# GpSimd multiplications with a second factor of 1.0, and a key bias by multiplication and addition, in a two-layer decoder kernel

## What is computed

```python
def trunk_layer(...):
    h = einsum('btd,de->bte', x, w_in)              # one projection, 4168 columns
    u = cc * ch                                     # mixer A: gated convolution, 256 channels
    conv = conv_w[0] * u_full[:, 0:t]
    for i in range(1, 3):
        conv = conv + conv_w[i] * u_full[:, i:i + t]
    y_a = cb * conv * silu(cg)
    y_b = stick_breaking(...) * silu(sg)            # mixer B: 6 heads x 64
    y_c = dsa_attend(...) * silu(dg)                # mixer C: 6 query heads, 2 kv heads
    x_new = layer_norm(ALPHA * x + concat(y_a, y_b, y_c) @ w_out)

def dsa_attend(...):                                # mixer C, per block of 128 queries
    score = ...                                     # indexer
    _, idx = top_k(where(admissible, score, -inf), 256)
    logits = where(valid, q @ gathered_k * HEAD_DIM ** -0.5, -inf)
    p = softmax(logits)
    o = p @ gathered_v
```

## Time and profile before

| what | value |
|---|---|
| time, median of 3 runs | 4671.03 us (4669.49 to 4673.32) |
| time of the profiled execution | 4666.6 us |
| span of the profiled execution | 4664.9 us |
| PE busy | 4315.7 us (93%) |
| DVE busy | 3508.5 us (75%) |
| ACT busy | 1737.3 us (37%) |
| POOL busy | 1472.1 us (32%) |
| POOL in the chain that ended last | 4% |

### The profile page before, as it was taken

The page is one execution under the profiler, slowest core; times in us unless marked ns, Lnnn a source line. Parts: engine busy times, 40 slices in busy tenths (PEclk is TensorE's granted clock), DMA queues, the critical chain, the costliest instruction groups (busy, mean ns, idle before and its releaser), DMA issues.

```text
span 4664.9 us, 79623 instructions
## 1 busy us (share of the span) xinstructions
PE 4315.7 (93%) x29678; PEld 2450.8 (53%) x29678; DVE 3508.5 (75%) x5659; ACT 1737.3 (37%) x2538; POOL 1472.1 (32%) x1393
## 2 busy tenths in 40 slices
PE   8988999999999898889999889999999998988899
PEld 6433545754466666454464235457544666655543
DVE  2785999999799774554537859999997997746445
ACT  3552212211266776330035522122112677754300
POOL 4310145400055795110033101454001647941100
PEclk9998999999899999999999989999999999999999
DMA  2102210211232003885211021112112320039832
GB/s 80 30 17 64 62 24 30 78 51 52 84 115 63 27 29 97 286 282 169 93 48 31 18 65 59 23 32 78 52 52 95 102 65 24 29 118 296 274 118 90
DMA packets 343763, 396.99 MB, mean 85 GB/s; under 512 B 100311, under 2 KB 264242, under 8 KB 340050
## 3 DMA queue, kind: packets, MB, share of 16 engines
q1 hardware_dynamic: 318034, 375.10, 25.6%
q10 hardware_dynamic: 25344, 16.79, 1.3%
HBM read 297.71 MB, written 94.14 MB: 84 GB/s over the span
## 4 chain that ended last, share of the span: by engine, by line
PE 72%; issue 6%; DVE 6%; ACT 6%; POOL 4%; SPq 2%; DMA 2%; ACTq 2%; DVEq 0%; PEldq 0%; POOLq 0%
PE banks L884 20%; PE banks L887 13%; PE banks L2127 10%; PE banks L328 5%; PE banks L368 4%; POOL arena L1577 2%; PE banks L1249 2%; PE banks L1211 2%; DVE arena L1362 2%; PE banks L1233 2%; PE banks L1823 1%; ACT arena L1559 1%; PE banks L1828 1%; PE banks L1513 1%; PE banks L1529 1%
## 5 line engine op out<-in xcount | busy, mean ns | idle before, releaser
L1037 DVE TENSOR_SCALAR_CACHE_REDUCE arena<-arena 128x1920 uint8<-128x1920 f32 (+13 forms) x896 | 1259.0, 1473 | 0.0
L884 PE MATMUL banks<-arena 128*128 128x512 f32 x2176 | 937.4, 592 | 0.0
L884 PEld LDWEIGHTS banks<-arena 128*128 128x128 f32 x2176 | 409.9, 189 | 520.4 <-issue 520.4
L887 PE MATMUL banks<-arena 128*128 128x384 f32 (+1 forms) x2048 | 620.0, 459 | 2.4 <-POOLq L142 2.4
L1362 DVE TENSOR_TENSOR_SCAN arena<-arena 128x129 f32<-128x129 f32 (+3 forms) x480 | 536.6, 1177 | 33.6 <-ACT arena L1273 23.2
L1577 POOL TENSOR_SCALAR arena<-arena 128x128 f32<-128x128 f32 (+14 forms) x180 | 512.1, 2861 | 13.8 <-DVE arena L1605 7.0
L467 DVE SCALAR_TENSOR_TENSOR arena<-arena 128x512 f32<-128x512 f32 (+3 forms) x532 | 403.6, 759 | 118.5 <-ACT arena L433 68.7
L887 PEld LDWEIGHTS banks<-arena 128*128 128x128 f32 x2048 | 380.1, 189 | 207.3 <-POOLq L142 2.6
L2127 PE MATMUL banks<-arena 128*128 128x512 f32 x1024 | 445.1, 597 | 12.3 <-DMA arena<-in_w_out 12.3
L1594 DVE CUSTOM_DVE_ANT_0 arena<-banks,arena 128x512 f32<-128x512 f32 (+3 forms) x480 | 269.4, 615 | 160.2 <-PE banks L1499 159.7
L433 ACT ACTIVATE arena<-banks 128x1024 f32<-128x1024 f32 (+3 forms) x304 | 278.3, 919 | 243.3 <-PE banks L368 130.8
(11 more groups left out here) (201 smaller groups left out, 5690.2 us busy)
## 6 DMA issues: line engine op xcount, KB each, us to landing
arena<-in_cache_sb_kv SPq DMA_DIRECT2D x256, 384.0 KB, 4.4
arena<-in_cache_dsa_kv SPq DMA_DIRECT2D x144, 128.0 KB, 4.3
arena<-in_x_prompt SPq DMA_DIRECT2D x32, 512.0 KB, 4.2
arena<-mixT SPq DMA_DIRECT2D x32, 512.0 KB, 4.0
arena<-xs SPq DMA_DIRECT2D x32, 512.0 KB, 4.4
arena<-in_cache_dsa_kv ACTq DMA_DIRECT2D x112, 128.0 KB, 4.6
arena<-in_w_in SPq DMA_DIRECT2D x8, 1536.0 KB, 7.5
out<-arena SPq DMA_DIRECT2D x64, 192.0 KB, 1.9
```

Of the source, the lines that this page charges most:

```text
L884: m = nc.tensor.matmul(bank[i % 4][:, :], W2[c % 2][:, k, j * P:(j + 1) * P], xT[:, k, t * FREE:(t + 1) * FREE], start=(k == 0), stop=(k = ...
L887: m = nc.tensor.matmul(bank[i % 4][:, 0:WD[name]], xT[:, k, t * P:(t + 1) * P], W2[c % 2][:, k, 0:WD[name]], start=(k == 0), stop=(k == KC ...
L1037: nc.vector.tensor_scalar(dummy[j % 2][:, 0:v.shape[-1]], v, thr[:, t:t + 1], 0.0, ALU.is_ge, ALU.add, accum_out=history[:, k, t:t + 1]).t ...
```

## The change

Three kinds of GpSimd instruction get other arithmetic; no instruction is added, removed or moved on any engine, and no wait, buffer or shape changes. The multiplications by one number per partition (L993, L997, L1577) had one operation and now have two: the product is multiplied by the constant 1.0. The key bias (L1331) had two operations, subtract 1.0 and multiply by 3.0e38, and now has two others: multiply by 3.0e38 and add -3.0e38. VectorE's own scaling (L1611) and its bias (`bias_end`) stay as they are.

```diff
@@ project_gpsimd
-                    nc.gpsimd.tensor_scalar(hc, u[:, 2:FREE + 2], cwT[:, b, 2:3], None, ALU.mult).then_inc(s_pp, 1)
+                    nc.gpsimd.tensor_scalar(hc, u[:, 2:FREE + 2], cwT[:, b, 2:3], 1.0, ALU.mult, ALU.mult).then_inc(s_pp, 1)
...
-                        nc.gpsimd.tensor_scalar(rC_flat[:, 0:FREE], u[:, k:FREE + k], cwT[:, b, k:k + 1], None, ALU.mult).then_inc(s_pp, 1)
+                        nc.gpsimd.tensor_scalar(rC_flat[:, 0:FREE], u[:, k:FREE + k], cwT[:, b, k:k + 1], 1.0, ALU.mult, ALU.mult).then_inc(s_pp, 1)
@@ stick_gpsimd
-                            nc.gpsimd.tensor_scalar(v, v, 1.0, -OUT_OF_REACH, ALU.subtract, ALU.mult)
+                            nc.gpsimd.tensor_scalar(v, v, -OUT_OF_REACH, OUT_OF_REACH, ALU.mult, ALU.add)
@@ sparse_gpsimd
-                    nc.gpsimd.tensor_scalar(lg[e % 4][:, g, 0:w], lg[e % 4][:, g, 0:w], ri[e % 4][:, g:g + 1], None, ALU.mult).then_inc(s_dn, 1)
+                    nc.gpsimd.tensor_scalar(lg[e % 4][:, g, 0:w], lg[e % 4][:, g, 0:w], ri[e % 4][:, g:g + 1], 1.0, ALU.mult, ALU.mult).then_inc(s_dn, 1)
```

## The result

The changed kernel takes 4619.15 us (median of 4 runs, 4615.22 to 4623.37), the kernel before, run beside it, 4672.17 us (4669.49 to 4675.64). The ratio is 0.9886, with a 95% interval of 0.9869 to 0.9903. The profiled execution has 4620.66 us and a span of 4618.9 us. The direction was forecast; the gain is twice the 27 us of the forecast, and the time lies under the range.

A forecast was written before the change was run, and what follows sets the result against it. GpSimd was taken to pace the sparse stage, with TensorE next. Sparse stages 25.4 us plus stick stage 2, projection 0, made 27 us off 4671.0: 4644 us, own range 4626 to 4656, 8-in-10 range 4625 to 4722.

The forecast's parts named there:

- the cheaper end: GpSimd's scalings: the two-operation form costs a third less than 2.50 ns a column; chosen by a small margin.
- The dearer end: GpSimd's scalings: the two-operation form costs 0.29 ns a column more, from the 128-wide bias piece; 0.84 was not believed.
- the argument from below: GpSimd adds two 512-wide tensors in 1087 ns but scales one in 1564, so another form can be cheaper.
- The sparse stage: Both layers' sparse stage: 12.7 us less a layer (9.7 paced stretch, 2 start, 1 negation), 25.4 us in all.
- 215.76 us: TensorE's busy time in layer 0's paced sparse stretch of 236.5 us, taken as fixed; 20.7 us were without work.
- the 11.0 us in which its transposes wait for ScalarE's copies stay: Paced sparse stretch: this TensorE wait remains as the order is unchanged, leaving 9.7 of 20.7 us to gain.
- The start: First 29 us of the sparse stage, narrow jobs: 2 us less, of the 6.7 that TensorE idles.
- L1600: VectorE's negation in the sparse stage, 1292 ns, on the way to ScalarE's exponential: shorter, 1 us a layer.
- Stick stage: Bias pieces beside VectorE's scans: 1 us a layer less, 2 in all, if pieces get a third shorter.
- Nothing: Rival for all changed scalings: the second factor costs and gives nothing, time stays 4671 us; chance 0.17.
- dearer: Rival in the paced sparse stretch: each column costs more, 10 to 50 us slower, chance 0.18; by more, 0.10.
- TensorE takes nearly all of it: Rival in the sparse stage: scalings cheaper but TensorE stays at 93%, gain 9 us, 4662 us; chance 0.08.

The follow-up runs named there:

- sparse_only: The kernel before with only the sparse stage's scaling L1577 given the second factor; 4627.08 us, ratio 0.9903.
- slow_half: The changed kernel with the old one-operation sparse scaling put back for the first kv group only; 4623.00 us, ratio 0.9895.
- doubled: The changed kernel with each sparse GpSimd scaling followed by a second quick one by 1.0 x 1.0; 4624.68 us, ratio 0.9905.
- no_bias: The kernel before without GpSimd's 38 bias pieces a layer, so the prompt's selection is not applied; 4648.33 us, ratio 0.9947.
- bias_late: The changed kernel with VectorE's negation folded into the maximum and 28 bias pieces a layer moved from stick to sparse stage; 4605.18 us, ratio 0.9852.
- bias_later: The changed kernel with VectorE's negation folded into the maximum and 36 of 38 bias pieces a layer moved to the sparse stage; 4600.72 us, ratio 0.9845.

## Why the prediction was right and wrong

**The bound.** Right. GpSimd paced the stretch between 1577 and 1813.5 us, and the three kernels that change its load (sparse_only, slow_half, doubled) move the time of that stretch only where the load fills the job. The projection stage didn't move.

**The price of two operations.** The choice of the cheaper end was right, both ends were not. I expected a third off; two thirds came off (2.50 to 0.84 ns a column). For the size of the gain this didn't matter: slow_half, with GpSimd's work in the stage 30% less (258 to 180 us), is nearly the forecast's own case, and it takes 4623 us and not 4644. The dearer end was wrong in a way that could have mattered. I took 0.29 ns more from the narrowest piece, by assuming that both forms have the same fixed 285 ns, and put aside the 512-wide piece at 1997 ns because scans ran beside it. The undisturbed price of such a pair is 2000 ns: the row that I didn't believe was the true one, and had the second multiplication fallen in this class, the kernel would have been some 140 us slower or more (an estimate from 84,800 columns a layer at 0.84 ns), not 50. That it didn't fall there was luck as much as reading: the argument from below showed that another form can be cheaper, and no row told which.

**The sparse stage: "215.76 us" as a floor, and "the 11.0 us in which its transposes wait for ScalarE's copies stay".** This is the step that failed. The stage was forecast at 12.7 us less a layer; it measured 22.4 in the profile of layer 0 and 19.6 in layer 1, and 42.6 for both layers timed alone against 25.4. The start was right (2 us forecast, 2.2 measured). The paced stretch was to give 9.7 us and 1 for L1600, and gave 17.7, in two parts. TensorE's idle time there fell by 12.5 us and not by 9.7, as the wait for the copies didn't stay at 11.0 us but fell to 3.1. And its busy time, below which I let nothing fall, fell by 5.2 us.

No matmul got shorter for that: in the paced stretch a transpose has 228 ns on average before and 227 now, a multiplication with values 277 in both, a 512-wide one of the logits 601 in both. What fell is the number of TensorE's waits of 0.15 us or more there, from 46 to 22. Matmuls that follow each other overlap in the profile (1292 transposes of 228 ns have 60.2 us of busy time), and the last one before a wait stands with its whole length. A wait so costs more than its own time, and the busy row carries the rest. This reading is argued from these rows; it fits the 5.2 us, some 0.2 for each of the 24 waits.

Why the wait for the copies went is argued too. In the kernel before, ScalarE's copies (L1559) waited for transposes that waited for GpSimd; when a job's scaling came, transposes and copies ran one behind the other in a burst. A wait for a third engine behind a paced one was part of the pace. That is taken from the two wait tables, and no run separates it further.

**L1600.** Put at 1 us a layer. Timed alone, with the slow scalings, taking the negation out gave 8.4 us in all, 4 a layer; in the changed kernel, without stalls, the same edit gave some 2 a layer in the profile.

**Stick stage.** Put at 2 us; 10.8 measured alone, some 7 at equal clock. This is the term that took the time out of the range: the range's low end had 41.4 us for the sparse stages, where 42.6 were measured, and 4 for this one. I had looked at the median of the scans, 1255 ns, and at TensorE's waits, when VectorE's busy share of the stage, 94%, says that little of what its scans lose could be made up. The comparison with the median was wrong by itself: the scans of 513 columns have 1339 ns without any piece beside them. That the pieces cost VectorE is shown by no_bias, bias_late and bias_later. That the slow form costs more in GpSimd's queue ("the next mask simply waits for ScalarE as before" was the forecast) is read from the traces at equal clock; for the scans behind the wide subtractions it is argued, and the rest of the 3.7 us of a layer stays open. A gain by a higher granted clock was in no term of the sum.

**The rivals.** "Nothing", "dearer" and "TensorE takes nearly all of it" didn't happen. The last was the same error as the failed step.

## What to carry to other kernels

When an engine paces a stage, take the bound of the next engine from its work and not from its busy and wait rows there: a part of both was made by the pace. A gain estimated by "its idle time less its other waits" was 60% of the measured one of the sparse stage here. Before a small gain is given to a change, compare runs or stretches of equal granted clock. On GpSimd write a scaling of float32 with a second factor of 1.0 or an addition of 0.0, and a subtraction as the addition of a negative. And where the instructions of a helper engine lengthen those of the engine that paces a stage, move them to a stage where neither is the bound, and don't merely space them out.

## What the hardware showed

- GpSimd's instruction with one tensor and two numbers has three prices at 128x512: 0.69 us for pairs made of multiplications and additions, 1.56 us for one multiplication, 2.00 us for pairs with a subtraction or a maximum. One operation costs more than twice as much as two.
- Which of the two numbers is the constant and which comes from a column in SBUF made no difference for two multiplications (691 to 697 ns with the constant first, 696 with it second).
- With the quick form, GpSimd's scaling of one tensor (696 ns) is cheaper than its addition of two (1089 ns), the order that the kernel before had reversed (1564 and 1087).
- VectorE's 128x2 negation and inverse took 1292 and 623 ns on average while GpSimd's scalings filled the stage, and 169 and 167 ns when they didn't.
- The bias pieces lengthen VectorE's scans about as much in the slow form as in the quick one: VectorE's busy time between the first and the last scan of layer 0 is 266.98 us without pieces, 275.36 with the quick ones (105.11 us of GpSimd) and 276.41 with the slow ones (140.66 us).
